# Two double norms of a two-block transformer kernel: where the squares are summed, and how many units run beside the norm

## What is computed

```python
h = memory_cross_attention(rmsnorm(x, norm_cross_pre[l]), rmsnorm(mem, mem_norm[l]), ...)
x = x + rmsnorm(h, norm_cross_post[l])
h = conv_glu_ffn(rmsnorm(x, norm_ffn_pre[l]), w_ffn_in[l], ffn_conv_w[l], ffn_conv_b[l], w_ffn_out[l])
x = x + rmsnorm(h, norm_ffn_post[l])
...
def conv_glu_ffn(xn, w_up, conv_w, conv_b, w_down):
    gu = xn @ w_up
    gate, up = jnp.split(gu, 2, axis=-1)
    gate = causal_dwconv(gate, conv_w) + conv_b.astype(gate.dtype)
    return (jax.nn.silu(gate) * up) @ w_down
```

## Time and profile before

| | us |
|---|---|
| median of 3 runs | 2170.08 |
| lowest and highest | 2169.40 and 2172.58 |
| span of the profiled execution | 2169.7 |
| TensorE busy | 2149.4 |
| VectorE busy | 983.0 |
| ScalarE busy | 847.1 |
| GpSimd busy | 893.9 |

### The profile page before, as it was taken

How to read it: one execution, slowest core, us unless ns; L and a number is a source line. 1 busy time by engine, 2 the same in 40 slices (tenths; PEclk the granted TensorE clock), 3 DMA queues, 4 the chain that set the end, 5 groups by cost and what they waited for, 6 DMA issues and landing times.

```text
span 2169.7 us, 27420 instructions
## 1 busy us (share of the span) xinstructions
PE 2149.4 (99%) x10303; PEld 1731.4 (80%) x10303; DVE 983.0 (45%) x1496; ACT 847.1 (39%) x1282; POOL 893.9 (41%) x684
## 2 busy tenths in 40 slices
PE   9999999999999999999999999999999999999999
PEld 7875787788888877767888888888888878888887
DVE  5755645576626143465432231346534655313221
ACT  6435645422222243565433232444333434423221
POOL 5431254154444443213444444433343315444443
PEclk9999999999999999999999999999999999999999
DMA  4222132133322332102222222322222213222223
GB/s 175 78 68 69 57 99 78 59 102 122 106 97 97 110 113 88 50 30 69 97 97 97 97 97 97 106 81 75 78 87 78 72 44 109 97 97 97 97 97 97
DMA packets 55109, 193.24 MB, mean 89 GB/s; under 512 B 6112, under 2 KB 6368, under 8 KB 54752
## 3 DMA queue, kind: packets, MB, share of 16 engines
q1 hardware_dynamic: 50112, 180.41, 25.0%
q10 hardware_dynamic: 4896, 11.41, 1.6%
HBM read 189.69 MB, written 2.10 MB: 88 GB/s over the span
## 4 chain that ended last, share of the span: by engine, by line
issue 52%; POOL 29%; PE 17%; POOLq 1%; DMA 0%; DVE 0%; ACT 0%; SPq 0%; ACTq 0%
POOL wl L552 29%; PE gemm_ps L587 6%; PE gemm_ps L588 6%; PE gemm_ps L589 6%; POOLq L549 0%; POOLq L561 0%; DMA x<-x_in 0%; DVE xl L2090 0%; ACT xh L1892 0%; ACT wh L1497 0%; PE turn_ps L729 0%; DVE x L2236 0%; SPq L526 0%; ACTq L1891 0%
## 5 line engine op out<-in xcount | busy, mean ns | idle before, releaser
L552 POOL TENSOR_TENSOR wl<-raw,wh 128x512 fp32r<-128x512 f32 x678 | 890.1, 1335 | 1258.0 <-ACT wh L1497 1248.8
L1497 ACT ACTIVATE wh<-raw 128x1024 fp32r<-128x1024 f32 x339 | 358.7, 1059 | 752.7 <-DMA raw<-w_in 742.1
L587 PE MATMUL gemm_ps<-xh,wh 128*128 128x512 f32 x1176 | 465.8, 396 | 0.0
L589 PE MATMUL gemm_ps<-xh,wl 128*128 128x512 f32 x1176 | 459.0, 390 | 0.0
L588 PE MATMUL gemm_ps<-xl,wh 128*128 128x512 f32 x1176 | 458.8, 390 | 0.0
L588 PE MATMUL gemm_ps<-arena_r,wh 128*128 128x512 f32 (+1 forms) x1088 | 417.0, 383 | 0.0
L587 PE MATMUL gemm_ps<-arena_r,wh 128*128 128x512 f32 (+1 forms) x832 | 320.0, 385 | 1.2 <-POOL wl L552 0.7
L589 PE MATMUL gemm_ps<-arena_r,wl 128*128 128x512 f32 (+1 forms) x832 | 317.4, 381 | 0.0
L587 PEld LDWEIGHTS gemm_ps<-xh,wh 128*128 128x128 f32 x1176 | 221.5, 188 | 49.6 <-issue 2.3
L588 PEld LDWEIGHTS gemm_ps<-xl,wh 128*128 128x128 f32 x1176 | 221.5, 188 | 47.4 <-issue 2.2
L589 PEld LDWEIGHTS gemm_ps<-xh,wl 128*128 128x128 f32 x1176 | 221.3, 188 | 46.7
(11 more groups left out here) (429 smaller groups left out, 2548.6 us busy)
## 6 DMA issues: line engine op xcount, KB each, us to landing
raw<-w_in SPq DMA_DIRECT2D x338, 512.0 KB, 3.4
arena<-na_in ACTq DMA_DIRECT2D x14, 256.0 KB, 2.7
out<-x ACTq DMA_DIRECT2D x8, 256.0 KB, 2.9
x<-x_in SPq DMA_DIRECT2D x6, 256.0 KB, 6.5
arena<-alibi_in ACTq DMA_DIRECT2D x6, 256.0 KB, 3.5
arena<-moba_in ACTq DMA_DIRECT2D x1, 1024.0 KB, 4.8
arena<-mem_in ACTq DMA_DIRECT2D x1, 1024.0 KB, 5.6
arena<-dist_in ACTq DMA_DIRECT2D x1, 896.0 KB, 4.5
```

The costliest lines, as they stand in the source:

```text
L552: m = pool.tensor_tensor(wl[:, k, half], raw[:, k, half], wh[:, k, half].bitcast(F32), ALU.subtract)
L587: pe.matmul(o, wh[:, n % RING, w], h[:, kt, 0:width], start=(kt == 0), stop=False)
L589: last = pe.matmul(o, wl[:, n % RING, w], h[:, kt, 0:width], start=False, stop=(kt == nkt - 1))
L1497: act.activation(wh[:, k % RING, :], raw[:, k % RING, :], ACT.Copy).then_inc(high_split, 1)
```

## The change

All of it lies in the two double norms.

- TensorE: `early_units` multiplies three units beside the norm in place of two. It sums no squares there. The fourth unit is cut in three, of 3, 3 and 2 blocks: behind the first piece stands one `token_sums` over summed squares, behind the second the spread.
- ScalarE: `prepare_summed` writes the square of block b to `y[:, b]` instead of `sq`, without waiting for anybody; behind block 2 it converts the fourth unit's weights.
- GpSimd: seven adds bring the eight squares into `y[:, 0]`, each waiting for its square and for the add before; behind the second of them it makes the fourth unit's low weights.
- TensorE: `highs_first` runs the fifth unit's 16 products with high weights when these are there, and waits for the low weights only then.

```diff
@@ gpsimd
+            def sum_squares(n0, base):
+                for b in range(1, KT):
+                    pool.wait_ge(block_squared, base + b + 1)
+                    if b > 1:
+                        pool.wait_ge(squares_summed, sums[0])
+                    pool.tensor_tensor(y[:, 0, :], y[:, 0, :], y[:, b, :], ALU.add).then_inc(squares_summed, 1)
+                    sums[0] += 1
+                    if b == 2:
+                        lows(n0 + 3, n0 + 4)
+            lows(0, FIRST["fup0"] + 3)
+            sum_squares(FIRST["fup0"], 0)
+            lows(FIRST["fup0"] + 4, FIRST["even_in"] + 3)
+            sum_squares(FIRST["even_in"], KT)
+            lows(FIRST["even_in"] + 4, UNITS)
@@ tensor, early_units
-                pe.wait_ge(unit_split, n0 + 2)
+                pe.wait_ge(unit_split, n0 + 3)
-                both = [(n, early_bank(n0, n)) for n in (n0, n0 + 1)]
+                beside = [(n, early_bank(n0, n)) for n in (n0, n0 + 1, n0 + 2)]
...
-                    take(square_ready)
-                    token_sums(sq[:, kt % 2, :], kt == 0, kt == KT - 1).then_inc(square_used, 1)
...
-                for n in (n0 + 2, n0 + 3):
-                    pe.wait_ge(unit_split, n + 1)
-                    piece(n, early_bank(n0, n), 0, 2, xh, xl)
-                    if n == n0 + 2:
-                        spread_tokens()
-                    piece(n, early_bank(n0, n), 2, KT, xh, xl)
+                last = n0 + 3
+                pe.wait_ge(unit_split, last + 1)
+                piece(last, early_bank(n0, last), 0, 3, xh, xl)
+                take(squares_summed, KT - 1)
+                token_sums(y[:, 0, :], True, True).then_inc(square_used, 1)
+                piece(last, early_bank(n0, last), 3, 6, xh, xl)
+                spread_tokens()
+                piece(last, early_bank(n0, last), 6, KT, xh, xl)
+
+            def highs_first(n):
+                o = gemm_ps[:, n % 2, :]
+                pe.wait_ge(high_split, n + 1)
+                pe.wait_ge(emptied, n - 3)
+                for kt in range(KT):
+                    w = slice(kt * P, (kt + 1) * P)
+                    pe.matmul(o, wh[:, n % RING, w], xh[:, kt, :], start=(kt == 0), stop=False)
+                    pe.matmul(o, wh[:, n % RING, w], xl[:, kt, :], start=False, stop=False)
+                pe.wait_ge(unit_split, n + 1)
+                for kt in range(KT):
+                    m = pe.matmul(o, wl[:, n % RING, kt * P:(kt + 1) * P], xh[:, kt, :], start=False, stop=(kt == KT - 1))
+                m.then_inc(unit_done, 1)
@@ scalar
+            def prepare_summed(gain, n0):
+                act.activation(eps[:, 3:4], eps[:, 0:1], ACT.Sqrt)
+                for b in range(KT):
+                    take(block_ready)
+                    act.activation(xh[:, b, :], x[:, b, :], ACT.Copy, scale=p_(gain, b)).then_inc(high_made, 1)
+                    act.activation(y[:, b, :], x[:, b, :], ACT.Square).then_inc(block_squared, 1)
+                    if b == 2:
+                        raise_to(n0 + 3)
+                take(square_used)
+                act.activation(token_std, turn_ps[:, 0, 0:T], ACT.Sqrt, bias=eps[:, 0:1],
+                               scale=1.0 / D).then_inc(std_ready, 1)
```

More of the change, by code:

```diff
@@ L453, in build @@
         square_used = sem("square_used")
+        block_squared = sem("block_squared")
+        squares_summed = sem("squares_summed")
         std_ready = sem("std_ready")
@@ L558, in _, with lows @@
             pool.wait_ge(rhs_ready, KT)
[L559 to L565, removed]
+            def lows(first, end):
+                rounds = (end - first) // RING
+                if rounds:
+                    with pool.Fori(0, rounds) as i:
+                        for n in range(first, first + RING):
+                            lower(n % RING, RING * i + (n + 1))
+                for n in range(first + RING * rounds, end):
+                    lower(n % RING, n + 1)
+            sums = [0]
+            def sum_squares(n0, base):
[12 more added lines that the diff above has]
+            lows(FIRST["even_in"] + 4, UNITS)
         @block.tensor
@@ L682, in early_units @@
                 keep_clock(2)
-                pe.wait_ge(unit_split, n0 + 2)
+                pe.wait_ge(unit_split, n0 + 3)
                 pe.wait_ge(emptied, n0)
-                both = [(n, early_bank(n0, n)) for n in (n0, n0 + 1)]
+                beside = [(n, early_bank(n0, n)) for n in (n0, n0 + 1, n0 + 2)]
                 def low_product(kt):
-                    take(square_ready)
-                    token_sums(sq[:, kt % 2, :], kt == 0, kt == KT - 1).then_inc(square_used, 1)
                     pe.wait_ge(rhs_ready, blocks_split[0] + kt + 1)
-                    for n, o in both:
+                    for n, o in beside:
                         m = pe.matmul(o, wh[:, n % RING, kt * P:(kt + 1) * P], xl[:, kt, :], start=False,
@@ L1271, in _ @@
             early_units(fup0, 3 * KT)
-            for n in (fup0 + 4, fup0 + 5):
-                next_unit(n, xh, xl)
+            highs_first(fup0 + 4)
+            next_unit(fup0 + 5, xh, xl)
             units(fup0 + 6, 2 * FF1_PARTS[0] - 6, xh, xl)
@@ L1291, in _ @@
             query_stat(0)
-            next_unit(even + 4, xh, xl)
+            highs_first(even + 4)
             query_stat(1)
@@ L1954, in _ @@
                     banks={KT - 2: score_ps[:, last, :], KT - 1: gemm_ps[:, last, :]})
-            prepare(x, "norm_ffn_pre", xh, lambda b: take(block_ready), tokens=True)
-            raise_to(FIRST["fup0"] + 3)
+            prepare_summed("norm_ffn_pre", FIRST["fup0"])
             gated()
@@ L1968, in _ @@
             prepare(y, None, None, stored_and_loaded, adds=KT - 2, tokens=True)
-            prepare(x, "attn_norm_e_2", xh, lambda b: take(block_ready), tokens=True)
             even, even_out = FIRST["even_in"], FIRST["even_out"]
-            raise_to(even + 3)
+            prepare_summed("attn_norm_e_2", even)
             for b in range(5):
```

## The result

| | before | after |
|---|---|---|
| median, us | 2170.08 (5 runs) | 2176.02 (5 runs) |
| lowest and highest | 2169.11 and 2172.58 | 2175.89 and 2180.84 |
| span of the profiled execution | 2169.7 | 2174.0 |

The ratio is 1.0033, with a 95% interval of 1.0022 to 1.0043: slower by 5.9 us, against 6.7 forecast.

A forecast was written before the change was run, and what follows sets the result against it. TensorE was taken as the bound, busy 2149.4 of 2169.7 us. Terms 5.6 - 0.5 + 1.6 = +6.7 gave a span of 2176.4, a median of 2176.8 us; range 2164.5 to 2184.

The forecast's parts named there:

- Holding: In the double norms each GpSimd instruction costs VectorE up to 1.04 us, making its last add of x 6.6 later.
- the walk through the norm: Step-by-step timing of VectorE and GpSimd in the first norm: adds of x 3 to 7 end at 416.0 to 428.1 us.
- The upper end by the prediction's reading of that rule: In a norm, VectorE's waits for GpSimd could each be a whole 1.25 us, at most 10 us instead of 8.3.
- Signs: Low parts about 1.7 us, GpSimd adds 1.6 or more, TensorE waits 1.2 in most rounds, seventh FFN unit about 5.
- The first norm: Norm ahead of the FFN: later spread starts the seventh unit at 456.7 against 451.12, 5.6 us lost.
- fifth unit's high products first: Running these before the low weights are there: worth nothing ahead of the FFN, 2.5 us ahead of the even mixer.
- The second norm: Norm ahead of the even mixer: seventh unit at 830.0 against 830.54, 0.5 us won.
- rival of a clock falling within the norms: TensorE's clock falls inside the norms too, two more falls costing up to 3.2 us: 2180; chance 0.18.
- Clock: One fall of TensorE's clock, for the 5.3 us stand before the seventh FFN unit: +1.6 us, ends 0 and 4.8.
- The adds don't hold: Rival: GpSimd's adds in the norms don't hold up VectorE; -5.4 us, 2164.5; chance 0.15.
- half hidden: Rival: half of GpSimd's delay to VectorE in the norms is hidden; median 2170, no change; chance 0.22.
- The mechanism of the slower side: The seventh FFN unit waits for VectorE; it costs as soon as the spread is later than 431.0 us.

The follow-up runs named there:

- even_only: The changed kernel with the change only at the norm ahead of the even mixer, the FFN norm as before: 2168.80 us, ratio to before 0.9997.
- adds_alone: The kernel before plus GpSimd adds in both double norms into a tile nobody reads, all else as before: 2171.71 us, ratio to before 1.0015.
- early_spread: The changed kernel with, at the FFN norm, the sum ahead of the fourth unit and the spread behind its second block: 2174.57 us, ratio to before 1.0024.
- four_banks: The changed kernel with four banks by turns instead of two in the first FFN part: 2169.20 us, ratio to before 0.9993.
- ffn_only: The changed kernel with the change only at the norm ahead of the FFN, the even mixer's norm as before: 2173.76 us, ratio to before 1.0024.
- before_banks: The kernel before with four banks by turns instead of two in the first FFN part: 2172.62 us, ratio to before 1.0013.
- no_adds: The changed kernel without GpSimd's adds of squares, so only block 0's square is summed: 2170.54 us, ratio to before 0.9994.
- rounded_two: The kernel before with squares rounded to fp32r in eight places, summed by TensorE with a rounded column of ones: 2162.91 us, ratio to before 0.9971.
- rounded_banks: Against before: three units beside the norm, four banks, no GpSimd adds, squares rounded to fp32r and summed on TensorE: 2162.59 us, ratio 0.9967.

## Why the forecast held

| step | forecast | after |
|---|---|---|
| adds to x, blocks 3 to 7, end behind the first scale | 8.8, 12.2, 15.6, 17.5, 20.9 | 8.73, 12.12, 15.50, 17.42, 20.83 |
| three units done | 24.4 | 24.50 |
| spread | 29.4 | 29.53 |
| seventh FFN unit | 49.5, stand 5.3 | 49.40, stand 4.79 |
| first products of the fifth even unit | 33.4 | 33.30 |
| seventh even unit | 47.8 | 49.48; 47.89 in even_only |
| clock, more than before | 1.6 | see below |

**Holding** was right in kind and size, since the walk through the norm gave each GpSimd instruction the price that the earlier trace rows show in another norm of the same kernel. The Trainium skill ("SBUF — State Buffer", "Who interferes with whom") calls the ports that VectorE and GpSimd share an exclusive lock, and has the order of issue decide who blocks. The order of arrivals in the timelines above agrees, and fits both prices. A GpSimd instruction of this shape takes 1.25 to 1.29 us alone. In after VectorE arrives when 1.24 are left (408.81 to 410.05) and waits 1.05; in adds_alone 0.90 are left, and it waits 0.76. The upper end by the prediction's reading of that rule, 1.25 us each, did not come. The prediction also told the rule without its exception: the section frees a VectorE instruction with one SBUF input only outside the 2-port modes, which it lists `tensor_scalar` as able to enter. In early_spread such an instruction took 1.50 us for 0.49 behind GpSimd, and the walk had no such term.

**Signs.** The low parts of 1.75 to 1.79 and the wait of 4.79 for VectorE came as named. TensorE's waits in the rounds were smaller, 0.29, 1.05, 1.04 and 0.95 us in four of eight where 1.2 in most was the sign, and of GpSimd's seven adds only three took over 1.6 us (1.73, 1.71, 1.73; the others 1.33 to 1.51).

**The first norm** came out at +5.53 against +5.6. That the fifth unit's high products first would be worth nothing there holds: the waits ahead of the stand were 0.53 and 1.10 us (0.7 and 1.5 forecast), and lay under it.

**The second norm** is the one place where the mechanism was right and the size off in the profile, +1.10 instead of -0.5. even_only puts it right: -0.49 without a clock fall behind its start. In the profiled execution of after the windows from 820 to 824 us, in the fifth even unit, lack 1.7 us of clock, and 1.10 less 1.7 is the forecast's -0.5 again, -0.6. That was my rival of a clock falling within the norms, and its case happened in part.

**Clock.** The stand cost one fall, as forecast, but a longer one: the windows from 452 to 458 us lack 3.4 us of clock, the first 0.4 of them still in the stand, where I had taken 1.6 from the fall at 781. That row of the ledger is +2.33. Over the timed runs the mean clock is 0.0020 lower than in before, by the spans above 2.8 us. This term was mis-sized, and that the whole came so near is in part luck: with 2.33 for it the forecast's own terms give 5.5 - 0.5 + 2.3 = 7.3 us, where the runs show 5.9.

**The rivals.** "The adds don't hold" and "half hidden" fell with the low parts of 1.79. The mechanism of the slower side, the seventh FFN unit waiting for VectorE, decided: four_banks takes that wait away and the loss with it. Two sums of the prediction are off without changing it: the rival without holding comes to 2169.7 - 5.4 + 0.4 = 2164.7, not 2164.5, and takes +0.3 for the first norm where the text ahead of it has +0.5; and the upper end of the range, 2184, is added up nowhere.

**What stays open.** The two norms account for +5.0 us in the profiles without clock (5.5 less 0.5), the runs for 5.9 less 2.8 of clock, 3.1. ffn_only shows it too: 3.9 us in the runs, 4.6 at equal clock, for 5.5 in the distance. A part of the rest is in my scale for the clock, which takes 1.4 us for each 0.001 wherever the clock is low. In the profile of after 4.2 us of lost clock lie where the distances show no cost of it (the start of both norms and the stand: ffn_only has 0.9 in the first of the distances, and 49.36 for 49.40), against 1.0 in before. The 3.2 between them are 0.0015 of the mean clock, 2.1 us by my scale, and 3.1 + 2.1 = 5.2. The same for ffn_only gives 5.1. This is an estimate from one profiled execution of each; no run shows it by itself.

## What to carry to other kernels

Before TensorE's small work is given to another engine, look at whose chain begins where that work ends: moving products ahead of a spread is no gain when the engine behind the spread has no slack, and a free bank can be worth more than the work moved. The price of a GpSimd instruction with SBUF operands is set by which VectorE instruction it meets, so it must be walked through in time, not multiplied. And look at the type of a small matmul before moving it: the cheapest edit here left it where it was and took four matmuls in place of eight.

## What the runs showed of the hardware

- A sum over 128 partitions of 512 columns in fp32 is eight matmuls in the trace and takes 0.81 us; with both operands rounded to fp32r it is four and takes 0.36.
- A VectorE tensor_scalar of 128x512 fp32 takes 0.49 us alone and 1.50 when a GpSimd instruction has just begun (early_spread), though it reads one SBUF tile; a scale with one operand in PSUM stays at 0.73.
- A low clock costs little where TensorE waits for others: between the first scale and the seventh FFN unit after and ffn_only lack 2.5 and 0.9 us of clock, and the distances are 49.40 and 49.36; before_banks and before lack 2.2 and 0, for 44.16 and 43.87.
- The clock falls in other places in each execution of the same code: at 211 to 217 us in before, no_adds, early_spread and rounded_two, and not at all there in after, ffn_only, even_only and rounded_banks. Over 75 runs of one kernel the mean clock went from 0.994 to 0.999, and the span by 6.8 us with it, more than the change costs.
